# The second ada vector of a two-block transformer kernel computed on TensorE from raw fp32 tiles

## What is computed

```python
c_act = jax.nn.silu(c)
for i in range(DEPTH):
    mod = c_act @ ada_w[i] + ada_b[i]
    sh1, sc1, g1, sh2, sc2, g2, sh3, sc3, g3 = jnp.split(mod, N_MOD, axis=-1)
    h = modulate(rms_norm(x, ln_ffn1[i]), sh1, sc1)          # h * (1 + sc) + sh
    x = x + 0.5 * g1[:, None, :] * swiglu(h, ffn1_wg[i], ffn1_wu[i], ffn1_wd[i])
    ...
```

## Time and profile before

| | us |
|---|---|
| median of three runs | 1806.57 |
| lowest and highest | 1805.0 and 1807.66 |
| span of the profiled execution | 1806.0 |
| TensorE busy in it | 1747.5 (97%) |
| VectorE busy in it | 1382.4 (77%) |
| ScalarE busy in it | 912.2 (51%) |

### The profile page before, as it was taken

One profiled execution on the slowest core, in us unless ns is written; L12 is line 12 of the kernel. 1 busy time (PEld: TensorE's weight loads), 2 busy tenths in 40 slices (PEclk: granted clock), 3 DMA queues, 4 the chain that ended last, 5 costly groups with the idle time before them and its releaser, 6 DMA issues. The chain is left out here.

```text
span 1806.0 us, 35803 instructions
## 1 busy us (share of the span) xinstructions
PE 1747.5 (97%) x14215; PEld 1709.8 (95%) x14215; DVE 1382.4 (77%) x1621; ACT 912.2 (51%) x1267; POOL 261.5 (14%) x423
## 2 busy tenths in 40 slices
PE   6999999999999999999999999899999998899999
PEld 5999999999999999989999998899999997699999
DVE  6767798687668877767967789769888898778555
ACT  3433377763335433456533366566444556655443
POOL 1411110011002011010110134411110121200000
PEclk9999999999999999999999999999999998999999
DMA  9988857459876888746697847335889492137450
GB/s 347 372 305 277 298 171 256 152 176 327 298 270 233 281 286 289 261 176 221 239 320 258 298 160 252 106 121 198 298 301 286 136 242 98 48 129 256 166 184 24
DMA packets 256071, 411.42 MB, mean 228 GB/s; under 512 B 17975, under 2 KB 200801, under 8 KB 255841
## 3 DMA queue, kind: packets, MB, share of 16 engines
q1 hardware_dynamic: 223032, 290.79, 49.2%
q0 software_dynamic: 32432, 119.04, 17.7%
q10 hardware_dynamic: 504, 0.18, 0.0%
HBM read 408.90 MB, written 2.63 MB: 228 GB/s over the span
## 5 line engine op out<-in xcount | busy, mean ns | idle before, releaser
L2678 DVE TENSOR_TENSOR lo<-raw,hi 128x2048 fp32r<-128x2048 f32 (+1 forms) x257 | 582.0, 2267 | 234.5 <-ACT hi L2512 234.0
L2512 ACT CAST hi<-raw 128x2048 fp32r<-128x2048 f32 (+1 forms) x266 | 498.4, 1876 | 387.2 <-PE dacc L2244 186.1
L2242 PE MATMUL up<-operand_hi,hi 128*128 128x256 f32 x1952 | 554.4, 284 | 3.6 <-DVE lo L2678 3.6
L2243 PE MATMUL up<-operand_lo,hi 128*128 128x256 f32 x1952 | 553.8, 284 | 0.0
L2244 PE MATMUL up<-operand_hi,lo 128*128 128x256 f32 x1952 | 553.6, 284 | 0.0
L2242 PEld LDWEIGHTS up<-operand_hi,hi 128*128 128x128 f32 x1952 | 375.9, 193 | 4.5 <-DVE lo L2678 4.4
L2243 PEld LDWEIGHTS up<-operand_lo,hi 128*128 128x128 f32 x1952 | 376.0, 193 | 0.0
L2244 PEld LDWEIGHTS up<-operand_hi,lo 128*128 128x128 f32 x1952 | 375.9, 193 | 0.0
L2242 PE MATMUL dacc<-act_hi,hi 128*128 128x256 f32 x1056 | 300.6, 285 | 3.4 <-DVE act_lo L2891 3.4
L2244 PE MATMUL dacc<-act_hi,lo 128*128 128x256 f32 x1056 | 299.8, 284 | 0.0
L2243 PE MATMUL dacc<-act_lo,hi 128*128 128x256 f32 x1056 | 299.2, 283 | 0.0
(11 more groups left out here) (432 smaller groups left out, 2784.4 us busy)
## 6 DMA issues: line engine op xcount, KB each, us to landing
ada<-in_ada_w_dram POOLq DMA_DIRECT2D x224, 512.0 KB, 6.0
raw<-in_ffn_wg_dram SPq DMA_DIRECT2D x88, 512.0 KB, 4.9
raw<-in_ffn_wu_dram SPq DMA_DIRECT2D x88, 512.0 KB, 5.3
raw<-in_ffn_wd_dram SPq DMA_DIRECT2D x88, 512.0 KB, 5.1
raw<-in_ffn_w_up_dram SPq DMA_DIRECT2D x88, 512.0 KB, 4.5
raw<-in_ffn_w_down_dram SPq DMA_DIRECT2D x46, 512.0 KB, 4.4
raw<-in_hg_w_in_dram SPq DMA_DIRECT2D x32, 512.0 KB, 6.0
raw<-in_attn_w_qkv_dram SPq DMA_DIRECT2D x24, 512.0 KB, 7.0
```

The lines of the kernel that those rows point to most:

```text
L2242: pe.matmul(o, stat[0], mov[0], start=start, stop=False, skip_group_check=True)
L2243: pe.matmul(o, stat[0], mov[1], start=False, stop=False, skip_group_check=True)
L2512: last = act.copy(put(slab(hi, s, SPL)), take(slab(raw, s, RAW)))
L2678: last = dve.tensor_tensor(put(slab(lo, s, SPL)), take(slab(raw, s, RAW)), put(slab(hi, s, SPL)).bitcast(F32), ALU.subtract)
```

## The change

Vector 1 is no longer accumulated on VectorE. `ada_product(k)` on TensorE multiplies tile k of it by c at once: eight fp32 matmuls with a raw 128x128 block of the tile as weights and the column k of c as the moving one, accumulated over k in PSUM; its semaphore `ada_direct` takes the place of steps 9 to 16 of `ada_step` in what waits for them (slabs 4 and 5, GpSimd's tiles of vector 2, `mod_vector(1)`). The tiles of vectors 0 and 1 are loaded in turn. The four filling matmuls go. The norm sums stand ahead of the parameter rows, the sum of vector 0 behind product 6 and in another bank. On VectorE the reciprocal comes after six steps, and the last two steps after the copies to `cols`.

```diff
-        def acc_of(v):
-
-            return view(8192, 9216) if v == 1 else ada_acc
...
-            if v >= 2:
-                eng.wait_ge(S["ada_step"], m - ATILES + 1 + KB * it)
+            if v == 2 and k < ATILES:
+                eng.wait_ge(S["ada_direct"], ATILES + k + 1)
+            elif v >= 2:
+                eng.wait_ge(S["ada_step"], m - ATILES + 1 - KB + KB * it)
             elif m >= ATILES:
                 eng.wait_ge(S["ada_step"], m % ATILES + 1)
...
+                elif s >= 4:
+                    sp.wait_ge(S["ada_direct"], 2 * s - 6)
                 elif s >= 2:
                     sp.wait_ge(S["ada_step"], 2 * s + 2)
...
-            for k in range(ATILES):
-                ada_load(sp, 0, k)
+            for k in range(2):
+                for v in range(2):
+                    ada_load(sp, v, k)
...
-                if i % 3 == 0 and ATILES + i // 3 < KB:
-                    ada_load(sp, 0, ATILES + i // 3)
+                if i % 3 == 0 and 2 + i // 3 < KB:
+                    for v in range(2):
+                        ada_load(sp, v, 2 + i // 3)
...
-            for k in range(KB):
-                ada_load(sp, 1, k)
-                if k == KB - 3:
+            for k in range(2 + -(-len(rows_plan[::2]) // 3), KB):
+                if k == KB - 2:
                     load(0, 0, up_src(phases[0], 0, 0))
+                for v in range(2):
+                    ada_load(sp, v, k)
             load(1, 0, up_src(phases[0], 0, 1))
...
+            def ada_product(k):
+
+                m = KB + k
+                pe.wait_ge(ada_early[m - ATILES] if k < ATILES else ada_first[m % ATILES], 16 if k < ATILES else 32)
+                for j in range(KB):
+                    last = pe.matmul(bank(misc, 1)[:, j:j + 1], ada_place(m)[:, j * P:(j + 1) * P], c_col[:, k:k + 1],
+                                     start=(k == 0 and j == 0), stop=(k == KB - 1), skip_group_check=True)
+                last.then_inc(S["ada_direct"], 1)
...
+            pe.wait_ge(S["c_ready"], 1)
+            ada_product(0)
+            ada_product(1)
             pe.wait_ge(S["x_loaded"], 16)
...
+            ada_product(2)
+            norm_sums(phases[0], wide=False)
+            for k in range(3, 6):
+                ada_product(k)
             pe.wait_ge(S["rows_loaded"], 16 * len(rows_plan))
...
-            ada_sum(0)
-            norm_sums(phases[0], wide=False)
-            keep_warm(bank(dacc, 0), WARM // 2)
             pe.wait_ge(S["rstd_done"], 1)
             spread(misc[:, SEQ:2 * SEQ], rstd).then_inc(S["spread"], 1)
-            ada_sum(1)
+            ada_product(6)
+            ada_sum(0, o=bank(up, 1)[:, SEQ:SEQ + KB])
+            ada_product(7)
...
-            for k in range(KB):
+            for k in range(6):
                 ada_tile(0, k)
-
+            dve.wait_ge(S["sqrt_done"], 1)
+            dve.reciprocal(rstd, rstd).then_inc(S["rstd_done"], 1)
             dve.wait_ge(S["cols_psum"], 2)
...
-            for k in range(KB):
-                ada_tile(1, k)
-            dve.wait_ge(S["sqrt_done"], 1)
-            dve.reciprocal(rstd, rstd).then_inc(S["rstd_done"], 1)
-            mod_vector(0)
+            for k in range(6, KB):
+                ada_tile(0, k)
             split_lo(0)
+            mod_vector(0, psum=bank(up, 1)[:, SEQ:SEQ + KB])
             mod_vector(1)
```

More of the change, by code:

```diff
@@ L205, in build @@
         names = """hi_done lo_done slab_used x_loaded rows_loaded const_done c_in cols_psum c_ready
-            ada_step ada_summed mod_done x_turned squared raw_hi_done raw_lo_done gate_scaled gate_full up_scaled presummed presummed_g sums_done sums_g_done
-            sqrt_done rstd_done spread gain_ready weight_ready row_kept scaled norm_hi norm_lo
+            ada_step ada_direct ada_summed mod_done x_turned squared raw_hi_done raw_lo_done gate_scaled gate_full up_scaled presummed presummed_g sums_done sums_g_done
+            sqrt_done rstd_done spread gain_ready row_kept scaled norm_hi norm_lo
             bank_done row_in out_turned out_scaled operand_ready x_done silu_done prod_done acthi_done
@@ L2363, in ada_sum @@
             def ada_sum(v, it=0, o=bank(misc, 1)):
-                pe.wait_ge(S["ada_step"], KB * (v + 1) + KB * it)
+                pe.wait_ge(S["ada_step"], KB * max(v, 1) + KB * it)
                 if v >= 1:
@@ L2368, in ada_sum @@
                 for k in range(KB):
-                    last = pe.matmul(o[:, k:k + 1], acc_of(v)[:, k * P:(k + 1) * P], ones[:, 0:1],
+                    last = pe.matmul(o[:, k:k + 1], ada_acc[:, k * P:(k + 1) * P], ones[:, 0:1],
                                      start=True, stop=True, skip_group_check=True)
                 last.then_inc(S["ada_summed"], 1)
+            def ada_product(k):
[5 more added lines that the diff above has]
+                last.then_inc(S["ada_direct"], 1)
             def keep_warm(o, n):
@@ L2550, in norm @@
                     act.wait_ge(S["gain_ready"], 2)
-                    act.activation(gain_weight[:, :], gain_sq[:, :], ACT.Identity, bias=eps_col).then_inc(S["weight_ready"], 1)
+                    act.activation(gain_weight[:, :], gain_sq[:, :], ACT.Identity, bias=eps_col)
                     split_hi(0)
@@ L2708, in ada_tile @@
                     dve.wait_ge(ada_full[m % ATILES], 16 * (m // ATILES + 1 - FIRST_ROUNDS) + 32 * it)
-                acc = acc_of(v)[:, :]
+                acc = ada_acc[:, :]
                 if k == 0:
                     if v > 1:
-                        dve.wait_ge(S["ada_summed"], v + it)
+                        dve.wait_ge(S["ada_summed"], v - 1 + it)
                     dve.tensor_scalar(acc, t, c, None, ALU.mult).then_inc(S["ada_step"], 1)
                 else:
-                    dve.wait_ge(S["ada_step"], m + KB * it)
+                    dve.wait_ge(S["ada_step"], (m if v < 2 else m - KB) + KB * it)
                     dve.scalar_tensor_tensor(acc, t, c, acc, ALU.mult,
@@ L2719, in mod_vector @@
             def mod_vector(v, it=0, psum=bank(misc, 1)):
-                dve.wait_ge(S["ada_summed"], v + 1 + it)
+                if v == 1:
+                    dve.wait_ge(S["ada_direct"], KB)
+                else:
+                    dve.wait_ge(S["ada_summed"], max(v, 1) + it)
                 if isinstance(it, int):
```

## The result

| | us |
|---|---|
| changed kernel, median of 4 runs | 1821.26 (1819.79 to 1823.71) |
| kernel before, median of 4 runs beside it | 1807.12 (1805.0 to 1810.48) |
| ratio, with 95% interval | 1.0073 (1.006 to 1.0086) |
| span of the profiled execution | 1822.1, before 1806.0 |

The changed kernel is 0.73% slower, some 13 us. The four runs spread by 4 us, and the profiled one is the slowest of them.

A forecast was written before the change was run, and what follows sets the result against it. TensorE's unbroken matmul chain was taken as the bound, so a first real product 13.5 us later moves the end one for one: 1806.57 us becomes 1820.0 us. Range of 8 in 10: 1813.5 to 1824 us.

The forecast's parts named there:

- the side that was named: Whole kernel: slower by more than 3.6 us, given 93%; faster was given 5%.
- the sum: Whole kernel: one term of +13.5 us on the median of 1806.57 us, giving 1820.0 us.
- the walk: TensorE's queue before the first real product, item by item: addition of vector 1 at 51.6 us instead of 38.14 us.
- The pace of a pass: Early TensorE stretch: lower clock of 1.2 GHz, 213 ns a pass, 3.42 us a product, 27.3 us for eight.
- the first rival: Early TensorE stretch: sustained work raises the clock, passes cost 105 ns, addition at 35.5 us, 1801.9 us; chance 5%.
- The wait for VectorE: Before the sum of vector 0: TensorE loses 1.2 us waiting for VectorE's last two tiles, done at 44.5 us.
- Two readings that the sum did not hang on: TensorE idle 2.4 us around 33 us before; lower clock in the first slab 3 us longer or shorter, worth 1.5 us.
- What was counted as hidden: Other queues before the first product: later rows, slabs, GpSimd's tiles and ScalarE's cast; none becomes last.
- The second: Rival: turning x raises the clock for a stretch on TensorE, worth 3 us, 1817.0 us; chance 12%.
- The third: Rival: weight loads of TensorE's products do not overlap, 5.3 us each, 15 us more, 1835 us; chance 3%.
- The fourth: Rival: after a later start, loaded slabs make the loss good, 1807 us; chance 2%.

The follow-up runs named there:

- e4: The kernel before with ten filling matmuls of 128 columns instead of four ahead of the spread; ratio to the kernel before 0.9997.
- e3: The changed kernel with the tile as moving operand (two 512-column matmuls) and parameter rows turned ahead of product 3; ratio to the kernel before 1.0029.
- e2: The changed kernel with the parameter rows turned ahead of products 3 to 5; ratio to the kernel before 1.0049.
- e5: e3 with the norm sums in wide form too and without the spread on TensorE; ratio to the kernel before 1.0022.
- e6: e5 with parameter rows turned ahead of the norm sums, products 3 to 7 in a row, slab 0 loaded behind the last ada tile; ratio to before 1.0023.
- e8: e6 with GpSimd's first four tiles of vector 2 held back until the row of vector 1 is turned; 1806.65 us, ratio to the kernel before 0.9985.
- e10: e8 with the products back in one-column form, eight matmuls a tile, no row turned; ratio to the kernel before 1.0028.
- e9: e8 with eight filling matmuls between the turning of the row and the first real product; ratio to the kernel before 0.9988.
- e7: e6 with eight filling matmuls of 128 columns at 3.3 us, ahead of product 0; ratio to the kernel before 1.0018.

## Why the prediction was right

1823.71 us in the profiled run, 1821.26 us at the median, against 1820.0 us forecast, inside the range and on the side that was named. The mechanism held too; what came out better than the sum, and what came out worse, partly cancel: the start was 0.5 us earlier than the walk had it, and 3.1 us were lost behind it in the profiled execution.

*The pace of a pass.* The step that decided was to trust the 333 ns of the load in the earlier trace rows over the clock of 1.00 in the earlier trace rows. e4 and e3 show clock records of 0.50 in such a stretch, and the products took 3.42 us each, within 0.02 us. Trusting the clock column would have led to the first rival.

*The walk through TensorE's queue.* Expected and found, in us: product 2 from 17.3 (16.8), norm sums from 20.7 (20.2), product 3 from 27.5 (27.1), parameter rows from 37.8 (37.2), sum of vector 0 from 44.5 (44.1), product 7 from 48.0 (47.5), addition of vector 1 at 51.6 (51.14). The half us comes from turning x, which took 3.44 us from its first load to the next product's, where I had put 3.7 us, from the first load to the end of the last matmul; it began 0.2 us early as well. Everything after kept that distance.

*The wait for VectorE.* 1.2 us forecast, 1.0 to 1.1 us found; e2 took it away and got 1.1 us.

*Two readings that the sum did not hang on.* The prediction gives TensorE 2.4 us of standing still around 33 us; the profile lists 1.0 us there, 1.3 us between its loads. And it lets the lower clock last 3 us longer or shorter in the first slab, which no row shows. Later runs without fillers have it from 2.8 us (e3, 44.3 to 47.1 us) to 6.1 us (e5, 42.5 to 48.6 us), so the allowance was about right, on the high side.

*What was counted as hidden.* Loads, slabs, GpSimd's tiles, ScalarE's cast: none became last, and no wait of TensorE is listed from 55 to 265 us. That only held because the products were slow. In e6, with fast ones, TensorE waited 8.6 us, and e8, which moves GpSimd's tiles alone, brought that down to 2.7 us.

*The rivals.* The first (clock up, faster) did not come: the loads of the products took 333 ns, at the median of all 128, from 6.7 to 51 us, though TensorE was busy nearly all the way. By the rule of the Trainium skill ("TensorE: Matmul & The Clock Gate", section "What's actually happening") sustained activity should have raised the clock; for one-column work these loads do not agree with it. What that rival would have given stays open: no run has the one-column products at full clock throughout. In e5, in the other form and with the clock up for most of the time, the start was 2.8 us later than before, where the rival had 2.6 us earlier; but the wait for the rows and the row's way over VectorE are in e5 and not in the rival. The second (a stretch at full clock after turning x) did not show in the profiled execution of the changed kernel, but it did in e10, where product 2 was 1.6 us shorter, and in e4. As e4 and the kernel before are one program up to there, that it stayed away here was partly luck, worth some 2 us; the rival had 12%, and e10's 1.6 us with some 0.3 us in the turned rows is less than the 3 us put on it. There the Trainium skill ("TensorE: Matmul & The Clock Gate", section "PE-mode transpose"), by which transposes don't raise the clock, differs from the measurement again: in e10 the load groups of product 2 and of the turned rows behind it are at full clock, after 3.46 us in which only x was turned, behind one-column products; in e4 the turning of x had 9 us of idle time ahead of it and nothing else. Whether these are the transposes that the page means, the trace does not say. The third (loads that don't overlap) is out: 213 ns from load to load. The fourth (the later start is made good) is out too: behind the start the changed kernel took 1769.4 us and the kernel before 1766.3 us, so nothing of the 13.0 us came back.

*What the prediction did not have* is the 3.1 us that the profiled execution lost behind the start. They are within the scatter of 6.8 us that this part shows over all profiled executions; the interval of the ratio, 11 to 16 us, holds the 13.0 us of the start.

## What to carry over

In these runs a queue of one-column matmuls was paid at the lower clock: look at the duration of one fixed form, not at a clock column that may have no record yet or at the busy share, and put the wide operand on the moving side where the work allows it. Work moved to an idle engine is free only up to that engine's idle time in front of the critical step, here some 10 us of holes after the first tile had landed (6.7 to 12.25, 15.9 to 19.0 and 32.4 to 33.7 us of the kernel before) against 27 us of products. And a transfer that waits for a step that you make faster starts sooner: hold it back where its bytes would stand ahead of something that is due.

## What the runs showed of the hardware

One fp32 tile of 128x1024 times one column costs the same in both forms at the same clock: 3.42 us as 16 one-column passes and 3.37 us as 4 passes of 512 columns (product 0 of e5) at the lower clock, 1.68 us and 1.71 us (product 3 of e6, 22.39 to 24.10 us) at the full one. The forms differ in what they do to the clock.

How soon the clock answered dense work at the very start differed between executions. The first wide matmul began between 6.83 and 7.03 us in e3, e5, e6, e8 and e9; the first half product at or near full pace (1.02 us busy, in e9 1.07 us) began at 9.87 us in e3, at 11.45 to 11.63 us in e5, e6 and e8, and at 12.04 us in e9. In e7, with fillers from 3.2 us on, it began at 9.67 us, only 0.2 us before e3.

The clock also rose behind stretches in which only x was turned, in some executions and not in others: at the end of the kernel before, in e4 and in e10, but not at the start of the kernel before and of the changed one.
